# Dilated heads' scores as two stacked fp32r products, and row sums from a column of ones, in a two-block transformer kernel

## The reference, cut to what matters

```python
proj = x @ w_in
a_in, b_in, c_in = split(proj)                      # A: q, k, v of 6 heads x 64
# A: three windows (128,1), (512,4), (2048,16), each a softmax; the three outputs are
#    weighted by the softmax of their log-sum-exps
s = einsum('q k', q, k) * 64 ** -0.5 + bias[t5_bucket(rel)];  p = exp(s - lse);  o = p @ v
# B: p1 - lam * p2, two softmaxes of 32-wide queries and keys, then a norm of the output
# C: causal softmax of 96-wide queries and keys (64 plus 32 with rotary positions)
heads = concat(o_a, o_b, o_c)
h = layer_norm(DEEPNORM_ALPHA * x + heads @ w_o)
x = layer_norm(DEEPNORM_ALPHA * h + (silu(h @ w_gate) * (h @ w_up)) @ w_down)
```

## Time and profile before

| | |
|---|---|
| time, median of 3 runs | 1942.44 us (1939.84 to 1943.55) |
| profiled execution: its own time / its span | 1941.8 us / 1940.0 us |
| TensorE, weight loads | busy 1895.1 us (98%), 1610.3 us (83%) |
| VectorE, ScalarE, GpSimd | 827.5 us (43%), 818.7 us (42%), 693.5 us (36%) |
| granted TensorE clock, mean | 0.995 of full speed |
| attention steps of the two layers | about 811 to 899 us, 1432 to 1520 us |

### The profile page before, as it was taken

One profiled execution on the slowest core, in us unless ns is written; L12 is line 12 of the kernel. 1 busy time (PEld: TensorE's weight loads), 2 busy tenths in 40 slices (PEclk: granted clock), 3 DMA queues, 4 the chain that ended last, 5 costly groups with the idle time before them and its releaser, 6 DMA issues.

```text
span 1940.0 us, 26619 instructions
## 1 busy us (share of the span) xinstructions
PE 1895.1 (98%) x10294; PEld 1610.3 (83%) x10294; DVE 827.5 (43%) x1871; ACT 818.7 (42%) x1573; POOL 693.5 (36%) x542
## 2 busy tenths in 40 slices
PE   8999989999899999999999999999999999999997
PEld 4897889878689888888988888888888898888886
DVE  3657866265567264576511110037267551111003
ACT  3321268363238465685332222126477432323222
POOL 0522502125430344212455454544420344544442
PEclk9999999999999999999999999999999999999999
DMA  9536322113230224211243433223320233332321
GB/s 283 166 109 217 106 45 55 44 44 116 80 87 34 90 88 118 85 34 55 77 109 87 109 87 130 87 79 109 110 82 23 69 84 109 87 106 90 130 87 44
DMA packets 199589, 181.95 MB, mean 94 GB/s; under 512 B 34823, under 2 KB 168957, under 8 KB 199465
## 3 DMA queue, kind: packets, MB, share of 16 engines
q1 hardware_dynamic: 193432, 168.93, 29.0%
q10 hardware_dynamic: 6032, 11.33, 1.9%
HBM read 178.10 MB, written 5.41 MB: 95 GB/s over the span
## 4 chain that ended last, share of the span: by engine, by line
PE 84%; DVE 5%; ACT 3%; issue 2%; POOL 2%; DMA 2%; SPq 0%; ACTq 0%; DVEq 0%
PE ps L1368 23%; PE ps L1370 22%; PE ps L1369 22%; PE ps L1962 3%; PE ps L1459 3%; PE ps L1879 3%; POOL w_lo L760 2%; DMA raw<-in_w_in 2%; PE ps L1426 2%; PE ps L1445 2%; PE ps L1980 2%; DVE acc L2172 1%; PE ps L1489 1%; ACT w_hi L815 1%; PE ps L1389 1%
## 5 line engine op out<-in xcount | busy, mean ns | idle before, releaser
L760 POOL TENSOR_TENSOR w_lo<-raw,w_hi 128x512 fp32r<-128x512 f32 (+2 forms) x507 | 668.5, 1351 | 1147.7 <-ACT w_hi L815 1147.6
L815 ACT ACTIVATE w_hi<-raw 128x1024 fp32r<-128x1024 f32 (+3 forms) x256 | 252.4, 1032 | 300.9 <-PE ps L1370 190.9
L1368 PE MATMUL ps<-g_hi,w_lo 128*128 128x512 f32 (+1 forms) x928 | 348.4, 375 | 1.4 <-POOL w_lo L760 1.4
L1369 PE MATMUL ps<-g_lo,w_hi 128*128 128x512 f32 (+1 forms) x928 | 347.5, 374 | 0.0
L1370 PE MATMUL ps<-g_hi,w_hi 128*128 128x512 f32 (+1 forms) x928 | 347.4, 374 | 0.0
L1368 PEld LDWEIGHTS ps<-g_hi,w_lo 128*128 128x128 f32 x928 | 174.7, 188 | 33.6 <-issue 1.7
L1370 PEld LDWEIGHTS ps<-g_hi,w_hi 128*128 128x128 f32 x928 | 174.7, 188 | 31.4
L1369 PEld LDWEIGHTS ps<-g_lo,w_hi 128*128 128x128 f32 x928 | 174.7, 188 | 30.8
L1368 PE MATMUL ps<-h_hi,w_lo 128*128 128x512 f32 (+1 forms) x496 | 181.8, 367 | 8.1 <-ACT cz L972 4.5
L2715 DVE TENSOR_TENSOR tmp_f<-ps,tmp_f 128x512 f32<-128x512 f32 x44 | 30.4, 692 | 370.7 <-PE ps L1370 370.7
L1369 PE MATMUL ps<-h_lo,w_hi 128*128 128x512 f32 (+1 forms) x496 | 175.7, 354 | 0.0
(11 more groups left out here) (310 smaller groups left out, 3426.8 us busy)
## 6 DMA issues: line engine op xcount, KB each, us to landing
raw<-in_w_in SPq DMA_DIRECT2D x30, 1024.0 KB, 5.4
raw<-in_w_mod SPq DMA_DIRECT2D x24, 1024.0 KB, 6.1
raw<-in_w_gate SPq DMA_DIRECT2D x44, 512.0 KB, 4.0
raw<-in_w_up SPq DMA_DIRECT2D x44, 512.0 KB, 5.3
raw<-in_w_down SPq DMA_DIRECT2D x22, 1024.0 KB, 4.9
raw<-in_w_out SPq DMA_DIRECT2D x8, 1024.0 KB, 11.6
strips<-bias_rows ACTq DMA_DIRECT2D x18, 256.0 KB, 3.1
raw<-in_w_in SPq DMA_DIRECT2D x16, 256.0 KB, 4.6
```

The costliest lines, as they stand in the source:

```text
L760: pool.tensor_tensor(w_lo[:, i % SPLIT, a:e], raw_of(what)[:, a:e], w_hi[:, i % SPLIT, a:e].bitcast(F32), ALU.subtract).then_inc(s_tile_lo ...
L815: act.activation(w_hi[:, i % SPLIT, a:b], raw_of(what)[:, a:b], ACT.Copy).then_inc(s_tile_hi.sem, s_tile_hi.nth((what, n)))
L1368: pe.matmul(o, lhs[1], rhs[0], start=first, stop=False)
L1369: pe.matmul(o, lhs[0], rhs[1], start=False, stop=False)
```

## The change

The operands of the dilated heads' scores change. `qa` is now fp32r: a head's 64 rows hold the high part of its queries and the other 64 rows, formerly zeros, the low part. ScalarE writes the high parts as before; VectorE computes the low parts from the product bank after those of `bk`, and the banks of i = 0, 1, 2 are released by VectorE, not ScalarE. GpSimd makes for each head `K_TWICE`, the rounded keys copied to both halves of a plane, and `K_LOW`, the rest of the keys in the head's own 64 rows. They lie in rows 3, 4 and 5 of `g_hi` and `g_lo`, used again from head to head, so each set waits for the last score that reads what lies there (`two_keys`). The score of a unit is the product of the stacked queries with `K_TWICE` plus the product of the high queries with `K_LOW`, into the same bank. Turning of chunk 1 now waits on ScalarE and VectorE for the last score of all, which comes before it in the list of steps.

The values of dilated and latent heads get a 65th column of ones per head (`va`, `vc`, filled by VectorE and GpSimd), so that the value product's 65th column is the row sum. Their exponentials no longer accumulate; their reciprocals are taken from that column, one for each unit. One score buffer moves to the place of `sin2`.

```diff
-        qa = put("qa", [P, A_HEADS, SEQ])
+        qa = put("qa", [P, A_HEADS, SEQ], F32R)
-        va = put("va", [P, XT, 384])
+        va = put("va", [P, XT, A_HEADS * VW])
...
-        sc2.append(at("sc2_4", [P, SEQ], names["w_lo"][0] + 4 * (TILE * UP_SLOT + XT * 384)))
+        sc2.append(at("sc2_4", [P, SEQ], names["sin2"][0]))
...
+        K_TWICE = [free_rows[r] for r in (("hi", 3), ("hi", 4), ("lo", 4), ("lo", 5), ("hi", 4), ("hi", 5))]
+        K_LOW = [free_rows[r] for r in (("lo", 3), ("hi", 5), ("lo", 4))]
...
+            def two_keys(y, h):
+
+                own, c = slice(HD * (h % 2), HD * (h % 2) + HD), h // 2
+                if h == 0:
+                    pool.wait_ge(s_proj.sem, s_proj.at((y, "a", 5)))
+                    before = ("c", 3)
+                else:
+                    before = (("c", 4), ("c", 5), ("c", 5), ("a", 2), ("a", 3))[h - 1]
+                pool.wait_ge(s_scores.sem, s_scores.at((y, SCORED_LAST[before])))
+                for half in range(2):
+                    pool.tensor_copy(K_TWICE[h][HD * half:HD * half + HD, :], ka[own, c, :]).then_inc(s_k_twice.sem, s_k_twice.nth((y, h)))
+                    pool.wait_ge(s_k_twice.sem, s_k_twice.at((y, h)))
+                pool.tensor_tensor(K_LOW[c][own, :], ka[own, c, :], K_TWICE[h][own, :].bitcast(F32),
+                                   ALU.subtract).then_inc(s_k_low.sem, s_k_low.nth((y, h)))
+                pool.wait_ge(s_k_low.sem, s_k_low.at((y, h)))
...
+                    pool.memset(vc[:].rearrange("p t (h d) -> p (t h) d", d=VW)[:, :, HD:VW], 1.0).then_inc(s_vc_ones.sem, s_vc_ones.nth(what[0]))
+                if what[1:] == ("o", 0, 1):
+                    pool.wait_ge(s_tile_lo.sem, s_tile_lo.at(splits[i - 1]))
+                    for h in range(A_HEADS):
+                        two_keys(what[0], h)
...
+                    if u["kind"] == "b":
+                        total = small[:, 1, i % 8:i % 8 + 1] if u["second"] else sums[:, u["sum"]:u["sum"] + 1]
+                        act.activation(p_, p_, ACT.Exp, bias=small[:, 0, i % 8:i % 8 + 1], scale=-1.0,
+                                       accum_out=total).then_inc(s_probs.sem, s_probs.nth((y, i)))
+                    else:
+                        act.activation(p_, p_, ACT.Exp, bias=small[:, 0, i % 8:i % 8 + 1], scale=-1.0).then_inc(s_probs.sem, s_probs.nth((y, i)))
...
                     if u["kind"] == "a":
-                        pe.wait_ge(s_padded.sem, s_padded.at(y))
-                    pe.matmul(ps[:, b, 0:u["n"]], u["q"], u["k"], start=True, stop=True).then_inc(s_scores.sem, s_scores.nth((y, i)))
+                        h = u["head"]
+                        own = slice(HD * (h % 2), HD * (h % 2) + HD)
+                        pe.wait_ge(s_a_lo.sem, s_a_lo.at((y, 2)))
+                        pe.wait_ge(s_k_low.sem, s_k_low.at((y, h)))
+                        pe.matmul(ps[:, b, 0:u["n"]], u["q"], u["k"], start=True, stop=False)
+                        pe.matmul(ps[:, b, 0:u["n"]], u["q"][own, :], K_LOW[h // 2][own, 0:u["n"]], start=False,
+                                  stop=True).then_inc(s_scores.sem, s_scores.nth((y, i)))
...
-                V.memset(qa[HD:P, 0::2, :], 0.0).then_inc(s_padded.sem, s_padded.nth(y))
-                V.memset(qa[0:HD, 1::2, :], 0.0).then_inc(s_padded.sem, s_padded.nth(y))
+                V.memset(va[:].rearrange("p t (h d) -> p (t h) d", d=VW)[:, :, HD:VW], 1.0).then_inc(s_va_ones.sem, s_va_ones.nth(y))
...
+                for i in range(3):
+                    for g in range(2):
+                        own, other = slice(HD * g, HD * g + HD), slice(HD - HD * g, P - HD * g)
+                        dve.wait_ge(s_a_hi.sem, s_a_hi.at((y, i, g)))
+                        V.scalar_tensor_tensor(qa[other, 2 * i + g, :], ps[own, AB[i], :], -HD ** -0.5, qa[own, 2 * i + g, :].bitcast(F32),
+                                               ALU.mult, ALU.subtract).then_inc(s_a_lo.sem, s_a_lo.nth((y, i)))
...
-                    elif u["opens"]:
-                        a = u["sum"] - u["i"]
-                        dve.wait_ge(s_probs.sem, s_probs.at((y, RANKS[last_of[u["kind"], u["head"]]])))
-                        step(V.reciprocal(recips[:, a:a + XT], sums[:, a:a + XT]))
                     dve.wait_ge(s_mixed.sem, s_mixed.at((y, r)))
+                    if u["kind"] != "b":
+                        step(V.reciprocal(total, ps[:, TURNED["unit", r], HD:VW]))
```

More of the change, by code:

```diff
@@ L44 @@
 QC = HD + ROPE
+VW = HD + 1
 EVEN, ODD = SEQ // 4 + 2, SEQ // 4
@@ L352, in _program @@
         s_proj = Signal(nc, ctx, seen, "proj")
-        s_padded = Signal(nc, ctx, seen, "padded")
+        s_a_hi = Signal(nc, ctx, seen, "a_hi")
+        s_a_lo = Signal(nc, ctx, seen, "a_lo")
+        s_k_twice = Signal(nc, ctx, seen, "k_twice")
+        s_k_low = Signal(nc, ctx, seen, "k_low")
+        s_va_ones = Signal(nc, ctx, seen, "va_ones")
+        s_vc_ones = Signal(nc, ctx, seen, "vc_ones")
         s_pt = Signal(nc, ctx, seen, "pt")
@@ L588, in unit @@
             def unit(kind, h, i, q, k, v, mask, at_col):
-                n = P * (i + 1)
-                return dict(kind=kind, head=h, i=i, n=n, q=q[:, P * i:P * i + P], k=k[:, 0:n], vs=[v[:, j, HD * h:HD * h + HD] for j in range(i + 1)],
+                n, w = P * (i + 1), HD if kind == "b" else VW
+                return dict(kind=kind, head=h, i=i, n=n, q=q[:, P * i:P * i + P], k=k[:, 0:n], vs=[v[:, j, w * h:w * h + w] for j in range(i + 1)],
                             mask=mask[:, 384 - P * i:SEQ], col=at_col + HD * h, second=False, first=False)
@@ L601, in units2 @@
             for h in range(A_HEADS):
-                others += [unit("a", h, i, qa[:, h, :], ka[:, h // 2, :], va, strip(h), 0) for i in (SLOT_ORDER if h < A_HEADS - 1 else (3, 2, 1, 0))]
+                others += [unit("a", h, i, qa[:, h, :], K_TWICE[h], va, strip(h), 0) for i in (SLOT_ORDER if h < A_HEADS - 1 else (3, 2, 1, 0))]
             u = [x for two in pairs[:EARLY // 2] for x in two]
@@ L610, in units2 @@
             u += others[done:]
-            ranks, seen_heads = [], set()
+            ranks = []
             for i, x in enumerate(u):
@@ L633, in _program @@
         LAST = len(RANKS) - 1
+        SCORED_LAST = {(u["kind"], u["head"]): i for i, u in enumerate(UNITS)}
         def turns(step):
@@ L1226, in a_out @@
                     if i < 3:
[L1227 to L1228 removed]
+                        for g in range(2):
+                            own = slice(HD * g, HD * g + HD)
+                            act.activation(qa[own, 2 * i + g, :], ps[own, AB[i], :], ACT.Copy, scale=-HD ** -0.5).then_inc(s_a_hi.sem, s_a_hi.nth((y, i, g)))
                     else:
@@ L1244, in exp2 @@
                     p_ = probs_of(i)[:, 0:u["n"]]
-                    total = small[:, 1, i % 8:i % 8 + 1] if u["second"] else sums[:, u["sum"]:u["sum"] + 1]
                     act.wait_ge(s_scored.sem, s_scored.at((y, i)))
-                    act.activation(p_, p_, ACT.Exp, bias=small[:, 0, i % 8:i % 8 + 1], scale=-1.0,
-                                   accum_out=total).then_inc(s_probs.sem, s_probs.nth((y, i)))
+                    if u["kind"] == "b":
[4 more added lines that the diff above has]
+                        act.activation(p_, p_, ACT.Exp, bias=small[:, 0, i % 8:i % 8 + 1], scale=-1.0).then_inc(s_probs.sem, s_probs.nth((y, i)))
                 act.wait_ge(s_lam_sums.sem, s_lam_sums.at(y))
@@ L1853, in _ @@
                         i = 2 * j + c
-                        fm(AB[i], (y, "a", j), w, c, s_proj.after((y, "a", i)), (y, "a", i))
+                        fm(AB[i], (y, "a", j), w, c, s_a_lo.after((y, i)) if i < 3 else s_proj.after((y, "a", i)), (y, "a", i))
                     left((y, "a", j))
@@ L1960, in mix @@
                         pe.wait_ge(s_proj.sem, s_proj.at((y, "vc", XT - 1)))
+                        pe.wait_ge(s_vc_ones.sem, s_vc_ones.at(y))
+                    if u["kind"] == "a":
+                        pe.wait_ge(s_va_ones.sem, s_va_ones.at(y))
                     for j, v in enumerate(u["vs"]):
-                        m = pe.matmul(ps[:, b, 0:HD], pt2[r % N_P][:, P * j:P * j + P], v, start=j == 0, stop=j == len(u["vs"]) - 1)
+                        m = pe.matmul(ps[:, b, 0:v.shape[1]], pt2[r % N_P][:, P * j:P * j + P], v, start=j == 0, stop=j == len(u["vs"]) - 1)
                     m.then_inc(s_mixed.sem, s_mixed.nth((y, r)))
```

20 lines of the change are left out of this document (14 added, 6 removed).

## The result

The changed kernel takes 1946.7 us (median of 16 runs, 1943.6 to 1948.7), the kernel before 1942.2 us (16 runs, 1939.8 to 1944.0). The ratio is 1.0023, with a 95% interval of 1.0016 to 1.0031: slower by 4.5 us, where 6.4 us of gain were forecast. The profiled execution took 1945.7 us, its span is 1943.8 us.

The account below looks back on a forecast made before the run. TensorE was taken to bound the kernel. Per layer 3.5 + 0.6 - 0.2 - 0.3 = 3.6 us, less 0.4, gave 3.2, or 6.4 us in all: from 1942.4 to 1936.0 us, range 1932 to 1941.

Parts of the forecast that it names:

- the price of the second product: Dilated scores on TensorE: second fp32r products cost 0.60 us a head, so a head saves 0.84 us.
- The other end: Dilated scores: if the second product cost as much as the first, 0.50 us a head saved, 6.0 us in all.
- Rival 4: Second product has 64 rows, weights loaded anew: 0.50 for 0.84 a head, 1938.6 us; chance 0.22 together with rival 1.
- the score's price: Dilated scores on TensorE: from 2.38 to 1.54 us a head, 5.0 us a layer saved.
- the small deductions: Per layer, off the gain: 0.2 us for row sums, 0.3 for slowed pairs, 0.4 for VectorE's squares and reductions.
- Row sums: Value products with 65 columns for 64: at most 0.4 us a layer more on TensorE, 0.2 taken.
- Low parts of the queries: Six VectorE combinations per layer, hidden while VectorE waits for the latent transposes: nothing; 4 us a layer without cover.
- rival 3: GpSimd's keys too late at heads five and six: 1.6 to 6.8 us lost, at 8 us sets 1946.8 us; chance 0.10.
- trio: GpSimd's two casts and one subtraction per head for the doubled keys: 2.8 to 7.0 us, 3.5 taken.
- Contention: VectorE's pair combinations slow beside GpSimd, 1.71 for 0.75 us: 0.3 us a layer lost, ends 0 and 1.2.
- rival 1: VectorE binds the middle stretch by reciprocals and slowed pairs: 1.8 us a layer, 1938.8 us; chance 0.22 together with Rival 4.
- VectorE's squares of the differential outputs: Last stretch: VectorE squares and reduces in one head's time, so 0.4 us of TensorE's 3.5 is held back.

Follow-up runs that it names:

- e1: The changed kernel with all 128 rows in the second product of each dilated score, by one more GpSimd copy per head and planes laid out anew: 1935.5 us.
- e2: The kernel with 128 rows in both products, but row sums accumulated by the exponentials as before and no column of ones: 1936.4 us.
- e3: The kernel before with only the row-sum part of the change, the column of ones and its reciprocals: 1941.8 us, ratio 0.9999.
- e5: The changed kernel with the second product of each dilated score left out: 1934.1 us, run once.
- e8: The changed kernel with the second product, of 64 rows, issued twice: 1955.2 us, run once.
- e9: The changed kernel with the first product, of 128 rows, issued twice: 1950.8 us, run once.

## Why the prediction was wrong, by its steps

**The step that failed** is the price of the second product: "I take 0.84 because the second product does follow one of its own kind". It doesn't. The rows it was read from are two products with 128 rows each; the new one has 64. The other end that I gave, as dear as a first product, was no bound either, since nothing in the earlier trace rows had a change of rows in it. Measured, the two changes cost 0.24 to 0.30 us of the pair and 0.03 to 0.07 us of the transposes behind it for each unit, 1.3 us a head against e1: 2.65 less 1.56, and 1.33 less 1.12 for the transposes. Against the kernel before the pairs cost 0.27 us more a head, where 0.84 less was forecast.

**Rival 4** had the mechanism in its words ("only 64 rows and its weights are loaded anew") and mis-sized it: 0.50 us saved a head, 1938.6 us. It left the first product and the transposes at their price. With the 0.27 and the 0.2 for transposes in its place, less 0.1 for value products (eight take 0.81 us, before 0.84), it would have said 0.4 us a head lost, 2.4 us a layer, 4.7 in all: what came.

**The rest of the score's price was right.** In e1, with 128 rows, a head takes 1.56 us (forecast 1.54), the whole kernel 1935.5 us (forecast 1936.0), and the attention is 3.5 and 3.6 us shorter in the two layers (forecast 3.2). That the total fits so well is in part luck: e1 is not the kernel that was forecast, and the small deductions below were not found where they were put.

**Row sums:** 0.2 us a layer was deducted; e1 against e2 shows nothing, and the 65-column products are no slower than the 64-column ones.

**Low parts of the queries:** they take 1.41 us for two and lie under the wait for TensorE, as said.

**GpSimd and rival 3:** a trio takes 2.6 us, below the 2.8 given as its lower end; the casts of 64 x 512 take 0.61 us each, like the copy of 32 x 512. Even e1's quartets (3.3 us) are never waited for. Rival 3 is out; that its 1946.8 us, for trios of 8 us, nearly meets the measured 1946.7 is chance.

**Contention:** the longest combination of a pair in the attention took 1.16 us in the changed kernel, not 1.71, and the wait of TensorE behind the one on the chain went from 0.22 to 0.31 us. The 0.3 us a layer could not be told apart. The prediction's "some 4 us less, as in rival 1" doesn't fit rival 1 as priced, which is 2.8 us less (1938.8 for 1936.0); neither came.

**VectorE, rival 1,** is not the reason for the loss (e3). Its busy time came as summed: 38.5, 13.6 and 20.5 us in the three stretches (forecast 38.6, 13.8, 20.6). It does hold back the gain: in e1 each head is 0.90 us shorter than before (875.84 to 880.20 against 5.26 us), 5.4 us for six, and 3.5 us arrive. TensorE's idle time in the attention rises from 1.4 us (87.26 - 85.86) to 3.0 us, and of it the waits for VectorE from 0.8 to 2.2 us, at two combinations and two divisions. But the reciprocals, by which rival 1 had it, are not what does it: e2 has 12 of them a layer for 48, waits for VectorE for 2.4 us, and its attention is as long.

```profile
811.02:894.74 83.72, 80.72 (x613) 71.41 (x613) 70.90 (x310) 65.43 (x169) 26.82 (x34) 1.00 0.11 33
```

The prediction held back 0.4 us for VectorE's squares of the differential outputs; the 0.58 us wait shown under e5 is at that place. What the attention would take without these waits was not tried.

## What to carry to other kernels

Count TensorE's changes between operands of 96 or 128 rows and operands of 64 or 32 (here in fp32r), not only its columns: fill up a small operand to 128 rows, even with terms that aren't needed, or put the small products side by side. Price a new product from a row with the same rows of operand and the same neighbours; where no row of the trace has such a pair of neighbours, the price is open upwards, and the longer form is the one to build first. Where one engine is full and another nearly so, expect a saving on the first to go through in part only: here 3.5 of 5.4 us, with VectorE busy for 85% of e1's attention.

## What the runs showed that was not expected

A score whose second product has 64 rows makes its first product 0.10 us longer (0.41 for 0.31 with 512 keys), the second 0.20 us (0.43 for 0.23), and the transposes behind it 0.05 us, though that second product has half the rows of the one that replaces it in e1. 96 rows cost what 128 do, 32 what 64 do. Both sides of a change pay: the product ahead of it is 0.10 us longer (e8, e9), whether it has 128 rows or 64. And one execution with a product less (e5) lost clock: 1.00 until about 885 us, 0.50 from 885.5 to 888.5, in the last stretch of the first layer. TensorE had waited 1.76 us for VectorE shortly before, but in the second layer it waited 1.64 us at the same place and kept full clock. It was seen once.
